# A fused attention stage on one Trainium2 core: scores of narrow units one unit ahead, recurrent gates in halves

## The reference, cut to what matters

```python
def block(i):                                  # diff_attention: 128 query rows
    sc = jnp.einsum('bhcqd,bhckd->bhcqk', qb, kt) * scale      # c = 0, 1
    sc = jnp.where(mask, sc, -jnp.inf)                         # causal
    p = jax.nn.softmax(sc, axis=-1)
    a = p[:, :, 0] - lam * p[:, :, 1]
    return jnp.einsum('bhqk,bhkv->bhqv', a, vt)
...
attn = rms_norm_2(attn, subln_w[l]) * (1.0 - lambda_init)
xc = causal_dwconv(xr, conv_rnn_w[l], conv_rnn_b[l])           # rg_lru on xc:
r = sigmoid(einsum(xb, wa) + ba);  ig = sigmoid(einsum(xb, wx) + bx)
log_a = -LRU_C * r * softplus(-lru_lambda);  a = exp(log_a)
u = sqrt(-expm1(2.0 * log_a)) * ig * x
h[t] = a[t] * h[t-1] + u[t]
```

## Time and profile before

| | us |
|---|---|
| median of 3 executions (lowest, highest) | 4888.94 (4885.94, 4891.41) |
| the profiled execution, and its span | 4889.43, 4887.6 |
| PE busy in the span | 4685.7 (96%) |
| the attention stage | about 3774 to 3984, 210 us |
| in it: PE, DVE, ACT busy | 143.3, 141.0, 136.4 |

### The profile page before, as it was taken

How to read it: one execution, slowest core, us unless ns; L and a number is a source line. 1 busy time by engine, 2 the same in 40 slices (tenths; PEclk the granted TensorE clock), 3 DMA queues, 4 the chain that set the end, 5 groups by cost and what they waited for, 6 DMA issues and landing times. The chain is left out here.

```text
span 4887.6 us, 68771 instructions
## 1 busy us (share of the span) xinstructions
PE 4685.7 (96%) x28888; PEld 3835.9 (78%) x28888; DVE 2548.3 (52%) x3698; ACT 1869.2 (38%) x3156; POOL 428.3 (9%) x347
## 2 busy tenths in 40 slices
PE   8999999999999999999999889899999679999999
PEld 5888877779889998989998644488777457888887
DVE  3245554546435555555555477555443755555543
ACT  3234443445235554555455433311233653111111
POOL 0000000000022322232322100000010000000000
PEclk9999999999989999999999999999999989999999
DMA  5334334334321011011100253343120021221232
GB/s 202 114 137 146 137 139 149 136 140 157 137 84 48 14 52 56 14 61 47 40 35 1 72 167 110 117 138 126 65 79 30 14 108 44 76 72 72 82 108 91
DMA packets 149074, 441.92 MB, mean 90 GB/s; under 512 B 16400, under 2 KB 46352, under 8 KB 131488
## 3 DMA queue, kind: packets, MB, share of 16 engines
q1 hardware_dynamic: 133712, 383.98, 22.2%
q0 software_dynamic: 9296, 32.58, 1.9%
q10 hardware_dynamic: 5760, 20.97, 1.2%
HBM read 294.86 MB, written 141.56 MB: 89 GB/s over the span
## 5 line engine op out<-in xcount | busy, mean ns | idle before, releaser
L172 PE MATMUL pr_ps<-uhl,w_split 128*128 128x512 f32 (+1 forms) x1520 | 585.8, 385 | 3.1 <-DVE w_split L144 2.2
L176 PE MATMUL pr_ps<-uhl,w_split 128*128 128x512 f32 (+1 forms) x1520 | 570.8, 376 | 0.0
L175 PE MATMUL pr_ps<-uhl,w_split 128*128 128x512 f32 (+1 forms) x1520 | 570.4, 375 | 0.0
L1475 DVE TENSOR_TENSOR b_G<-b_ps,cst 128x512 fp32r<-128x512 f32 x480 | 327.6, 689 | 326.3 <-PE b_ps L1258 325.7
L137 ACT ACTIVATE w_split<-share 128x2048 fp32r<-128x2048 f32 x64 | 122.6, 1915 | 703.2 <-DVE ou_vc L3173 271.5
L172 PEld LDWEIGHTS pr_ps<-uhl,w_split 128*128 128x128 f32 x1520 | 286.5, 189 | 81.7 <-issue 29.2
L1134 ACT ACTIVATE b_X<-b_ps 128x512 fp32r<-128x512 f32 x400 | 240.2, 600 | 240.9 <-PE b_ps L1258 240.9
L175 PEld LDWEIGHTS pr_ps<-uhl,w_split 128*128 128x128 f32 x1520 | 286.7, 189 | 55.8 <-issue 5.8
L176 PEld LDWEIGHTS pr_ps<-uhl,w_split 128*128 128x128 f32 x1520 | 286.5, 188 | 52.5
L1138 ACT ACTIVATE b_Y<-b_ps 128x512 fp32r<-128x512 f32 x480 | 286.5, 597 | 88.6 <-PE b_ps L1258 88.6
L1258 PE MATMUL b_ps<-b_G,b_Y 128*128 128x128 f32 x1920 | 305.9, 286 | 13.5 <-DVE b_G L1475 13.2
(11 more groups left out here) (475 smaller groups left out, 10114.1 us busy)
## 6 DMA issues: line engine op xcount, KB each, us to landing
w_ring<-in_w_in SPq DMA_DIRECT2D x41, 1024.0 KB, 5.1
proj<-pr_stage SPq DMA_DIRECT2D x160, 256.0 KB, 2.0
share<-in_w_up SPq DMA_DIRECT2D x24, 1024.0 KB, 4.7
ar<-share SPq DMA_DIRECT2D x32, 512.0 KB, 2.8
b_AR<-ar SPq DMA_DIRECT2D x16, 1024.0 KB, 12.0
pr_raw<-proj SPq DMA_DIRECT2D x48, 256.5 KB, 3.5
ada<-in_ada_w SPq DMA_DIRECT2D x24, 512.0 KB, 5.5
ff<-ou_vc ACTq DMA_DIRECT2D x24, 512.0 KB, 2.6
```

The costliest lines, as they stand in the source:

```text
L172: mm = nc.tensor.matmul(dst, a[0], b[0], start=start, stop=False)
L175: nc.tensor.matmul(dst, a[0], b[1], start=False, stop=False)
L176: return nc.tensor.matmul(dst, a[1], b[0], start=False, stop=stop)
L1475: L[x]["dve"].done(V.tensor_tensor(Gs[x][:], heads(x, 0), rep(K(f"lev{m}"), 4), ALU.mult), f"{n}.G{m}")
```

## The change

Three things are changed, all in `attend`.

1. Where the scores lie and when they are made. Units t = 1 and t = 3 now lie in banks 1 and 3, units t = 0 and t = 2 stay in banks 0 and 2 (they are at most 512 columns wide), so `sc(n+1)` is put ahead of `tr(n-1)` in iterations t = 0, 1 and 2. In heads 2 and 3, where `flip` uses banks 1 and 3, `sc` of t = 1 stays in its own iteration and waits for `head_out`. The other units keep their place.
2. The gate products use bank 5 alone, one half (512 columns) at a time, in four iterations t = 1 to 4, each after `tr` and `av`. Each half waits for ACT's tanh of the half before it. Bank 5 also holds the transposes of units of more than 512 columns, so `tr` of t = 4 waits for the last half's tanh.
3. The order on the other two engines. On DVE, in iterations t = 1 to 3 the two row minima stand before `soft(n-1)`, and `admit` moves from t = 3 to t = 5. On ACT, the four tanh halves stand in iterations 1, 2, 3 and 4, one each.

```diff
+        def scored(n, c):
+            t = units[n][1]
+            first = HALF if t in (1, 3) else 0
+            return S[:, c, first:first + (t + 1) * P]
...
                     if n >= 1:
-                        pe.wait_ge(exp_ready, 2 * n)
-                    if t == 4:
-                        pe.wait_ge(th_x, h + 1)
+                        pe.wait_ge(exp_ready, 2 * (n - 1) if 1 <= t <= 3 else 2 * n)
+                    if t == 1 and h >= 2:
+                        pe.wait_ge(head_out, h - 1)
...
                 def tr(n):
                     h, t = units[n]
                     pe.wait_ge(diff, n + 1)
                     if n >= 1:
                         pe.wait_ge(aT_ready, n)
+                    if t == 4:
+                        pe.wait_ge(th_x, 2 * h + 2)
...
-                def gates(k, x):
-                    if x == 0:
+                def gates(k, x, half):
+                    if x == 0 and half == 0:
                         pe.wait_ge(conv, k + 1)
-                        if k >= 2:
-                            pe.wait_ge(head_out, k - 1)
                         if k == 0:
                             pe.wait_ge(w_in, 32)
                         else:
-                            pe.wait_ge(exp_ready, 16 * k)
+                            pe.wait_ge(aT_ready, 8 * k)
+                    elif x == 0 or half == 0:
+                        pe.wait_ge(th_a, 2 * k + 1 + x)
                     else:
-                        pe.wait_ge(th_a, k + 1)
-                    for half in range(2):
-                        mm = nc.tensor.matmul(ps[:, 1 + 2 * half], wg[:, x, k], xc[k % 2][:, half * HALF:(half + 1) * HALF], start=True, stop=True)
-                    mm.then_inc(gate_x if x else gate_a, 1)
+                        pe.wait_ge(th_x, 2 * k + 1)
+                    nc.tensor.matmul(ps[:, 5], wg[:, x, k], xc[k % 2][:, half * HALF:(half + 1) * HALF],
+                                     start=True, stop=True).then_inc(gate_x if x else gate_a, 1)
...
-                    sc(n)
-                    if t == 1:
-                        gates(h, 0)
-                    if t == 2:
-                        gates(h, 1)
+                    if t in (0, 4, 5, 6, 7) or t == 1 and h >= 2:
+                        sc(n)
                     if t == 0 and h >= 2:
                         pe.wait_ge(exp_ready, 2 * n)
                         flip(h - 2)
+                    elif t < 3:
+                        sc(n + 1)
                     if n >= 1:
                         tr(n - 1)
                     if n >= 2:
                         av(n - 2)
+                    if 1 <= t <= 4:
+                        gates(h, (t - 1) // 2, (t - 1) % 2)
...
                     if t == 1:
-                        open_a(h)
+                        open_a(h, 0)
...
                     if t == 2:
-                        open_x(h)
+                        open_a(h, 1)
                         decay(h)
                     if t == 3:
+                        open_x(h, 0)
                         decay2(h)
                         bend(h)
-                    if t == 4 and h:
-                        norm(h - 1)
+                    if t == 4:
+                        open_x(h, 1)
+                        if h:
+                            norm(h - 1)
...
-                    if n >= 1:
+                    if n >= 1 and not 1 <= t <= 3:
                         soft(n - 1)
                     peak(n, 0)
                     peak(n, 1)
+                    if 1 <= t <= 3:
+                        soft(n - 1)
...
-                    if t == 3:
-                        admit(h)
...
                     if t == 5:
+                        admit(h)
```

More of the change, by code:

```diff
@@ L2526, in sc @@
                             r = slice(64 * c, 64 * c + 64)
-                            nc.tensor.matmul(S[:, c, b:min(w, b + HALF)], qk[r, h, t * P:(t + 1) * P],
+                            nc.tensor.matmul(scored(n, c)[:, b:min(w, b + HALF)], qk[r, h, t * P:(t + 1) * P],
                                              qk[r, 4 + h, b:min(w, b + HALF)], start=True, stop=b + HALF < w)
                     for c in range(2):
-                        nc.tensor.matmul(S[:, c, t * P:w], id_r[:], mask_r[:], start=False, stop=True).then_inc(scores, 1)
+                        nc.tensor.matmul(scored(n, c)[:, t * P:w], id_r[:], mask_r[:], start=False, stop=True).then_inc(scores, 1)
                 def tr(n):
@@ L2608, in exp @@
                         act.wait_ge(turned, n - 1)
-                    A(p[:, n % 2, c, 0:w], S[:, c, 0:w], ACT.Exp, scale=-1.0, bias=nb[:, n % 2, c:c + 1],
+                    A(p[:, n % 2, c, 0:w], scored(n, c), ACT.Exp, scale=-1.0, bias=nb[:, n % 2, c:c + 1],
                       accum_out=sm[:, n % 2, c:c + 1]).then_inc(exp_ready, 1)
@@ L2643, in end, with open_a, open_x @@
                     A(out[:, h % 2, HALF:T], flat_at(h, 1), ACT.Copy, scale=sub_w[:]).then_inc(head_out, 1)
-                def open_a(k):
-                    act.wait_ge(gate_a, k + 1)
+                def open_a(k, half):
+                    act.wait_ge(gate_a, 2 * k + half + 1)
                     if k:
                         act.wait_ge(tn, k)
[L2649 to L2653, removed]
+                    A(ra[:, half * HALF:(half + 1) * HALF], ps[:, 5], ACT.Tanh, scale=0.5, bias=hb[:, 0, k:k + 1]).then_inc(th_a, 1)
+                def open_x(k, half):
+                    act.wait_ge(gate_x, 2 * k + half + 1)
                     if k:
                         act.wait_ge(scan, k)
-                    A(ix[:, 0:HALF], ps[:, 1], ACT.Tanh, scale=0.5, bias=hb[:, 1, k:k + 1])
-                    A(ix[:, HALF:T], ps[:, 3], ACT.Tanh, scale=0.5, bias=hb[:, 1, k:k + 1]).then_inc(th_x, 1)
+                    A(ix[:, half * HALF:(half + 1) * HALF], ps[:, 5], ACT.Tanh, scale=0.5, bias=hb[:, 1, k:k + 1]).then_inc(th_x, 1)
                 def decay(k):
-                    act.wait_ge(th_a, k + 1)
+                    act.wait_ge(th_a, 2 * k + 2)
                     if k:
@@ L2745, in peak @@
                         dve.wait_ge(exp_ready, 2 * n - 2)
-                    V.tensor_reduce(nb[:, n % 2, c:c + 1], S[:, c, 0:w], AX.X, ALU.min).then_inc(nb_ready, 1)
+                    V.tensor_reduce(nb[:, n % 2, c:c + 1], scored(n, c), AX.X, ALU.min).then_inc(nb_ready, 1)
                 def soft(n):
@@ L2789, in admit @@
                 def admit(k):
-                    dve.wait_ge(th_x, k + 1)
+                    dve.wait_ge(th_x, 2 * k + 2)
                     dve.wait_ge(conv, k + 1)
```

## The result

| | before | after |
|---|---|---|
| median of 10 executions, us | 4888.25 (4885.23 to 4892.82) | 4900.1 (4896.16 to 4905.48) |
| ratio to before | | 1.0024, 95% interval 1.0016 to 1.0032 |
| profiled execution, its span, us | 4889.43, 4887.6 | 4900.43, 4898.7 |

The change costs 11.9 us. The prediction was +8, and 4897 for the time: 4 us short as a difference, 3 as a time, and 4900.1 lies inside its range of 4888 to 4904, at the upper end of the branch that it held likeliest (+5 to +11). The prediction took 0.2% as the line between same and slower and gave "same" 0.59, "slower" 0.37. The measured ratio is 0.24% above one, and its interval, 0.16% to 0.32%, holds that line: which side of it the change falls is not settled.

The account below looks back on a forecast made before the run. No single engine bounds attention; each head is DVE, PE and ACT pieces in series. Head 0 -1.7, head 1 +1.6, heads 2 and 3 +4.0 each sum to +7.9, say +8: 4897 us, range 4888 to 4904.

Parts of the forecast that it names:

- the branch that it held likeliest: Whole kernel 5 to 11 us slower, PE's clock low in most heads; chance 0.5.
- head 0: First head, no norm or flip: scores of t = 2 and 3 ready early, gain 1.7 us or 0.9.
- head 1, first gate tanh: ACT's gate work starts 0.7 us earlier; 1.5 us more saved if the clock stayed up.
- heads 2 and 3, first gate tanh: Starts 1.7 us later in each: scores of t = 1 wait for `end`, minima precede `soft`.
- (c): First gate tanh to square root, ACT nearly gapless, 20.8 us; predicted cost 0.5 order plus 1.8 clock a head.
- The three pieces: In series: DVE gapless from square root to t = 0 minima, then PE, then ACT; together a head's cost.
- The rival itself: Clock falls already at t = 1 of heads 2 and 3: +2.8 us each, 4897 to 4903; chance 0.18.
- (a+b): From a square root to the next head's first gate tanh: the DVE piece, then the PE piece.
- The clock's part: At t = 3 in (c): low clock after PE's 3.0 us idle costs 1.8 us a head, 0 to 2.7.
- Faster by look-ahead: In t = 1 to 4, PE's waits for exponentials are removed: 4877; chance 0.04.
- the halves cost nothing: Gate halves and banks have no effect, even heads 2 and 3's 1.7 us hidden: 4889; chance 0.06.
- the sum without the term: Rival that PE's clock stays up in (c), dropping 1.8 us a head: +2.6, 4892; chance 0.22.

Follow-up runs that it names:

- the second profile: The changed kernel run and profiled once more, nothing altered; 4900.26 us, ratio to before 1.0026.
- e7: Changed kernel plus one unread PE product at t = 0 of heads 1 to 3 and one at t = 1 of heads 2 and 3; 4894.06 us.
- e3: Changed kernel with scores of t = 1 in heads 2 and 3 back in old banks, t = 2 scores in their own iteration; 4895.15 us.
- e1: Changed kernel with DVE's old order restored: the combined map ahead of the row minima in t = 1 to 3; 4890.57 us.
- e2: Changed kernel plus four unread PE products in the idle stretch at t = 3 of heads 1 to 3; 4891.34 us.
- e5: Kernel before plus only the gate halves, with their tanh halves and `admit` moved to match; 4881.84 us, ratio to before 0.9985.
- e4: Changed kernel with the edits of e1 and e3 together; 4887.19 us, ratio to before 0.9994.

## Why the prediction was right, and where it was off

| term, us | predicted | measured, after less before |
|---|---|---|
| head 0 | -1.7 (or -0.9) | +0.3; -1.1 in the second profile |
| head 1, first gate tanh | -0.7 | -0.8 |
| heads 2 and 3, first gate tanh | +1.7 each | +3.2, +3.9 |
| (c), heads 1 to 3 | +2.3 each | +2.1, +1.9, +1.2 |
| tail | 0 | +0.3 |
| sum | +7.9 | +12.0 |

- **The three pieces.** Right. The waits of rows 2 did not decide: PE's wait for exponentials fell from 26.5 to 22.8 us in the trace of after, and the time rose. The waits of PE's transposes for the combined map, 27.2 us before by the list of waits, are now 34.7:

```profile
PE at_ps L2545 <- DVE at_p L2768: 34.7, 14, 4.9
...
PE at_ps L2532 <- ACT at_p L2616: 22.8, 13, 3.9
```

- **Heads 2 and 3, the order.** Right: 1.7 predicted, 1.8 and 1.5 by e7, with the scores waiting 1.61 us for ACT's copy.
- **Heads 2 and 3, the clock.** This is the term that was mis-sized: the sum has it at nothing, and it measured 1.4 us in head 2 and 5.0 in head 3 (e7 against the changed kernel). It stood among the rivals with 0.18, because head 2 of before had kept the high clock over two gaps of 1 us. The rival itself had the place wrong in part. It listed a new gap of 1.6 us ahead of the scores of t = 1 and priced the products of t = 7 and the gate half. But the slow rows begin with the transposes of t = 7, ahead of that gap, and in head 2 they end before it; e3 has no such gap and its transposes are slow too. Only head 3 had slow products of t = 7 (3.04 us), and the gate half took 1.02 us, the fast time, in both. Whether the gap of 1.6 us has a part in head 3 is open: where the transposes ahead of it were fast, the rows behind it were fast in e1 head 3 and e2 head 2, and the products of t = 7 slow (2.95 us) in e2 head 3, as the rival had it. Head 3 of before, which the prediction does not mention here, had the slow start already, with an (a+b) 2.5 us over head 2's:

```profile
3917.88 1.97 PE L2538 MATMUL at_ps<-cst,at_p 128*128 128x128 f32 x8 [1.04 <-DVE at_p L2760]
3919.64 3.19 PE L2549 MATMUL at_ps<-share,at_aT 128*128 128x128 f32 x14
```

With 1.5 us for head 2 and 2.4 for head 3 the sum comes to 11.8. That this meets the 12.0 is in part luck: head 0 missed by 2.0 us one way and (c) by 1.8 the other.
- **Idle stretches and the clock.** All seven stretches of over 2.5 us that the prediction had were followed by the low clock; the new traces have others that were not. The eight score instructions of t = 6 came after 2.71 to 2.73 us of idle in all three heads of after; they took 3.36 us in head 1 and 1.77 in heads 2 and 3, the time that they also took after 1.83 us in before:

```profile
3850.93 3.36 PE L2532 MATMUL at_ps<-qk 64*128 64x512 f32 x8 [2.71 <-ACT at_p L2616]
...
3902.26 1.77 PE L2532 MATMUL at_ps<-qk 64*128 64x512 f32 x8 [2.71 <-ACT at_p L2616]
```

In e7, head 2, the same 2.87 us at t = 3 were followed by fast transposes (0.55 us) and a slow gate half (1.72). So the length of the gap before them does not settle by itself how fast the products behind it are.
- **Piece (c).** Right in place and near in size. The idle stretch was predicted as 3.0 us and is 2.87, the slow transposes follow it in all heads of both profiles, and ACT waits twice before its third tanh, 1.6 to 1.8 us in all where 2 to 3 had been named. The clock's part was set at 1.8 us; e2 puts it at 0.6 at least and at 1.5 by the estimate above. So it was set too high by 0.3 to 1.2, and the rest of the 2.0 measured in heads 1 and 2, 0.5 to 1.4, is the order's, set at 0.5. Head 3 shows +1.2 because (c) of before was itself 0.7 us longer there (20.45 against 19.7), with its scores of t = 5 at 2.93 us where heads 1 and 2 have 1.56.
- **Head 1.** The first tanh 0.7 us earlier, as worked out from ACT's unchanged order. The 1.5 us for a high clock came in the second profile (24.95 against 26.59) and not in the first.
- **Head 0.** Wrong in size. The first tanh came 0.5 us earlier, but in the first profile PE was slow into the second gate half (1.45 us on PE's timeline in place of 1.02) and ACT waited 0.97 us for it. In the second profile it took 1.02 and the wait was 0.53; even there the saving is 1.1 us and not 1.7.
- **The rivals.** Faster by look-ahead: nothing of it showed, the stage got longer. That the halves cost nothing is true in itself (e5), but not what that rival claimed.
- **The rule on small clock penalties.** By the runs the low clock costs some 6 us at t = 0 and 1 of heads 2 and 3 and 2 to 4.5 in (c), 8 to 11 us of 4900. That is under 1%, as the Trainium skill (TensorE: Matmul & The Clock Gate, Part 1) says. But the sum without the term was 4892, 8 us short of what was measured.

Open: what brings the clock down at t = 0. The gap behind the flip is the same 1.04 us whether the transposes after it are slow (after, e1 head 2, e3) or fast (before head 2, e1 head 3, e2, e5). It was not settled either why the clock at t = 0 of head 1 is high in one execution and low in the next of the same kernel, nor why it differs between heads 2 and 3 in e4. What is shown is that it was low in heads 2 and 3 in both profiles of the changed kernel, and high there in the one of e7, with products added.

## What to carry to other kernels

Before pricing a wait, find the pieces in series and which engine has no gap in each; a wait beside them can shrink and the kernel get slower. Work put ahead in a queue must not carry a wait of its own: scores one unit ahead moved the wait for an old copy, and the minima, in front of what the chain needed. Where a reorder opens a gap of some microseconds on PE, price the products behind it at the low clock as well as the high; read every head of the trace before, as one of them may already show the slow case. Try the parts of a change apart: here one gained 6 us and the other lost 18.

## What was not expected of the hardware

- Adding work to PE made the changed kernel faster, though not faster than before: four products of 0.9 us in three heads, 8.8 us less (e2); five products in all, 6.0 us less (e7).
- Low-clock stretches can repeat to 0.02 us between executions (heads 2 and 3 of the changed kernel) while the one of head 1 comes and goes, worth 1.6 us.
- The clock's effect of an edit can show far from it: e2 changed only t = 3, and in its profile most of the gain lay at t = 0 and 1 of the heads after it.
- An idle stretch of 2.71 us on PE was followed by the low clock in one head and by the high clock in another of the same execution.
